# Block products in all four feed-forward blocks, beside the modulation's sums, and the sums over h in mid-turn

## The reference

```
mod = c_act @ mod_w[i] + mod_b[i]                    # 9 rows of 1024 per layer: shift, scale, gate
h = modulate(rmsnorm(x, ffn_norm_w[i, 0]), sh1, sc1)
g, u = jnp.split(h @ w_gu, 2, axis=-1)               # w_gu: 1024 x 5632, so 2816 gate and 2816 up columns
x = x + FFN_HALF * g1[:, None, :] * ((jax.nn.silu(g) * u) @ w_down)
```

## Time and profile before

| | |
|---|---|
| median of 3 runs | 2077.13 (2076.99 to 2077.41) |
| profiled execution, its own time | 2075.79 |
| its span, first to last instruction | 2074.0 |
| TensorE busy | 2056.9 (99% of the span) |
| VectorE busy | 1286.6 (62%) |
| ScalarE busy | 840.3 (41%) |
| DMA | 300.66 MB, mean 145 GB/s |

### The profile page before, as it was taken

One profiled execution on the slowest core, in us unless ns is written; L12 is line 12 of the kernel. 1 busy time (PEld: TensorE's weight loads), 2 busy tenths in 40 slices (PEclk: granted clock), 3 DMA queues, 4 the chain that ended last, 5 costly groups with the idle time before them and its releaser, 6 DMA issues.

```text
span 2074.0 us, 28876 instructions
## 1 busy us (share of the span) xinstructions
PE 2056.9 (99%) x11146; PEld 1741.0 (84%) x11146; DVE 1286.6 (62%) x1985; ACT 840.3 (41%) x1317; POOL 5.6 (0%) x34
## 2 busy tenths in 40 slices
PE   9999999999999999999999999999999999999998
PEld 6888888987878888888888988988888788899887
DVE  6555566687877755555566677664237975766433
ACT  4232222367667743322222344333125843434221
POOL 0000000000000000000000000000000000000000
PEclk9999999999999999999999999999999999999999
DMA  8455566444344323355467533334331113333322
GB/s 336 181 192 202 197 239 234 141 136 136 117 119 140 107 82 120 145 202 194 182 235 247 197 113 102 102 102 151 104 110 61 55 61 122 102 102 141 123 92 72
DMA packets 84253, 300.66 MB, mean 145 GB/s; under 512 B 9008, under 2 KB 11952, under 8 KB 82480
## 3 DMA queue, kind: packets, MB, share of 16 engines
q1 hardware_dynamic: 83856, 299.01, 42.1%
q10 hardware_dynamic: 288, 0.13, 0.0%
HBM read 292.68 MB, written 6.42 MB: 144 GB/s over the span
## 4 chain that ended last, share of the span: by engine, by line
PE 96%; DVE 2%; DMA 1%; ACT 0%; SPq 0%; issue 0%; DVEq 0%; ACTq 0%
PE bank L259 30%; PE bank L261 30%; PE bank L260 30%; PE bank L1223 1%; DMA raw<-w_stream 1%; PE bank L1878 1%; PE bank L1232 1%; PE bank L1913 1%; PE bank L1893 1%; PE bank L1227 1%; DVE x_trunk L859 0%; DVE w_lo_sb L254 0%; PE bank L1214 0%; PE bank L1211 0%; PE bank L388 0%
## 5 line engine op out<-in xcount | busy, mean ns | idle before, releaser
L259 PE MATMUL bank<-h_hi,w_hi_sb 128*128 128x512 f32 (+1 forms) x1924 | 711.4, 370 | 5.9 <-DVE w_lo_sb L254 4.7
L260 PE MATMUL bank<-h_lo,w_hi_sb 128*128 128x512 f32 (+1 forms) x1924 | 702.8, 365 | 0.0
L261 PE MATMUL bank<-h_hi,w_lo_sb 128*128 128x512 f32 (+1 forms) x1924 | 702.8, 365 | 0.0
L254 DVE TENSOR_TENSOR w_lo_sb<-raw,w_hi_sb 128x1024 fp32r<-128x1024 f32 (+1 forms) x326 | 387.1, 1195 | 119.5 <-ACT w_hi_sb L249 119.3
L259 PEld LDWEIGHTS bank<-h_hi,w_hi_sb 128*128 128x128 f32 x1924 | 363.0, 189 | 70.9 <-DVE w_lo_sb L254 6.8
L261 PEld LDWEIGHTS bank<-h_hi,w_lo_sb 128*128 128x128 f32 x1924 | 362.8, 189 | 59.0
L260 PEld LDWEIGHTS bank<-h_lo,w_hi_sb 128*128 128x128 f32 x1924 | 363.2, 189 | 56.3 <-issue 0.2
L249 ACT ACTIVATE w_hi_sb<-raw 128x1024 fp32r<-128x1024 f32 (+1 forms) x326 | 326.1, 1028 | 146.8 <-PE bank L261 142.0
L259 PE MATMUL bank<-a_hi,w_hi_sb 128*128 128x512 f32 (+1 forms) x912 | 324.1, 355 | 0.0
L261 PE MATMUL bank<-a_hi,w_lo_sb 128*128 128x512 f32 (+1 forms) x912 | 323.4, 355 | 0.0
L260 PE MATMUL bank<-a_lo,w_hi_sb 128*128 128x512 f32 (+1 forms) x792 | 289.4, 365 | 0.0
(11 more groups left out here) (263 smaller groups left out, 2139.1 us busy)
## 6 DMA issues: line engine op xcount, KB each, us to landing
raw<-w_stream SPq DMA_DIRECT2D x356, 512.0 KB, 3.6
mod_raw<-w_mod SPq DMA_DIRECT2D x144, 512.0 KB, 4.4
sums<-sums_rows SPq DMA_DIRECT2D x7, 1024.0 KB, 9.2
decays<-decay_rows SPq DMA_DIRECT2D x8, 768.0 KB, 4.0
first_mod<-w_mod SPq DMA_DIRECT2D x10, 512.0 KB, 15.5
x_rows<-x_trunk SPq DMA_DIRECT2D x4, 1024.0 KB, 4.9
x_trunk<-x_rows SPq DMA_DIRECT2D x4, 1024.0 KB, 6.6
first_mod<-w_first SPq DMA_DIRECT2D x3, 1024.0 KB, 18.6
```

The source lines that it names most:

```text
L254: nc.vector.tensor_tensor(w_lo_sb[:, s, 0:width], raw[:, s, 0:width], w_hi_sb[:, s, 0:width], ALU.subtract).then_inc(w_lo, 1)
L259: nc.tensor.matmul(ps, s_hi, m_hi, start=start, stop=False)
L260: nc.tensor.matmul(ps, s_hi, m_lo, start=False, stop=False)
L261: return nc.tensor.matmul(ps, s_lo, m_hi, start=False, stop=stop)
```

## The change

All four blocks get blocked turns: blocks 0 and 1 from turn 4 to turn 9, six turns each, with the mod_blocks at the places `blocks(0)` to `blocks(3)`. `token_whole` moves into the middle of a turn, behind that turn's first two `prep_lo`. In blocks 2 and 3 it stays in the same turn, and `token_sums` goes to the middle of the turn after it. In blocks 0 and 1 they stand in the middle of turns 1 and 2. Blocks 0 and 1 now also store x and fetch it back; the fetch stands in `gu_turn(9)`, behind the first slab load and the first modulation load. The loops of these blocks are written out turn by turn, and the gate and up slabs of the blocked turns are stored in the order that blocked turns read (gate 1, gate 0, up 0, up 1).

```diff
-BLOCKED_FROM = {2: 2, 3: 3}
+BLOCKED_FROM = {0: 4, 1: 4, 2: 2, 3: 3}
...
         def token_whole(dve, k):
             t0 = BLOCKED_FFN.index(k)
             dve.wait_ge(x_put, 32 * (t0 + 1))
+            dve.wait_ge(h_lo_ready, (h_before[0] + 8, h_before[2] + 16, h_before[4] + 8, h_before[6] + 16)[k])
...
                 elif k in BLOCKED_FROM and i == BLOCKED_FROM[k] - 1:
                     preps(0, True)
+                    if mod0 is None:
+                        token_sums(dve, k)
                     leave(0)
                     sum_s3(dve, k, n0, i + 1)
...
                 else:
                     preps(0, True)
+                    if k in BLOCKED_FROM and i == BLOCKED_FROM[k] - 2 - int(mod0 is not None):
+                        token_whole(dve, k)
+                    if k in BLOCKED_FROM and i == BLOCKED_FROM[k] - 2 and mod0 is not None:
+                        token_sums(dve, k)
                     leave(0)
...
                     turn(i, v, part, first)
-                    if i == BLOCKED_FROM[k] - 2:
-                        token_whole(dve, k)
-                        token_sums(dve, k)
...
+            def slabs_and_mods(k, n0, m0, made):
 
                 def gu_turn(i, blocks):
                     for u in range(2):
                         for q in range(2):
                             load_slab(sp, 4 * i + (n0 + 2 * u + q), (n0 + 2 * u + q) % RING)
                             if blocks:
-                                load_mod(sp, 4 * i + (m0 - 4 * halved + 2 * u + q), q)
-
-                if halved:
-                    gu_turn(0, False)
-                with sp.Fori(int(halved), 2 * MOD_GU + int(halved)) as i:
+                                load_mod(sp, 4 * i + (m0 - 4 + 2 * u + q), q)
+                            if i == BLOCKED_TO - 1 and u == q == 0:
+                                fetch_x(k)
+
+                gu_turn(0, False)
+                put_x(made)
+                for i in range(1, 2 * MOD_GU + 1):
                     gu_turn(i, True)
```

More of the change, by code:

```diff
@@ L2218, in _, with put_x, fetch_x @@
                 load_slab(sp, n, n % RING)
-            def slabs_and_mods(n0, m0, halved):
+            x_flat = x[:, :, :].rearrange("p j t -> p (j t)")
+            x_halves = (slice(0, DT * T // 2), slice(DT * T // 2, DT * T))
+            def put_x(made):
+                sp.wait_ge(t_ready, made)
+                for w in x_halves:
+                    sp.dma_start(x_rows[:, w], x_flat[:, w]).then_inc(x_put, 16)
+            def fetch_x(k):
+                sp.wait_ge(part_done, 6 * blocked_before(k, BLOCKED_TO))
+                sp.wait_ge(x_put, 32 * (BLOCKED_FFN.index(k) + 1))
+                for w in x_halves:
+                    sp.dma_start(x_flat[:, w], x_rows[:, w]).then_inc(x_back, 16)
+            def slabs_and_mods(k, n0, m0, made):
                 def gu_turn(i, blocks):
@@ L2227, in gu_turn @@
                             if blocks:
-                                load_mod(sp, 4 * i + (m0 - 4 * halved + 2 * u + q), q)
-                if halved:
-                    gu_turn(0, False)
-                with sp.Fori(int(halved), 2 * MOD_GU + int(halved)) as i:
+                                load_mod(sp, 4 * i + (m0 - 4 + 2 * u + q), q)
[4 more added lines that the diff above has]
+                for i in range(1, 2 * MOD_GU + 1):
                     gu_turn(i, True)
-                if not halved:
-                    gu_turn(2 * MOD_GU, False)
                 def down_turn(i, last):
@@ L2247, in slabs_and_mods @@
                     down_turn(i, i == 1)
-            x_flat = x[:, :, :].rearrange("p j t -> p (j t)")
-            x_halves = (slice(0, DT * T // 2), slice(DT * T // 2, DT * T))
-            def put_x(made):
-                sp.wait_ge(t_ready, made)
-                for w in x_halves:
-                    sp.dma_start(x_rows[:, w], x_flat[:, w]).then_inc(x_put, 16)
-            def fetch_x(k):
-                sp.wait_ge(part_done, 6 * blocked_before(k, BLOCKED_TO))
-                sp.wait_ge(x_put, 32 * (BLOCKED_FFN.index(k) + 1))
-                for w in x_halves:
-                    sp.dma_start(x_flat[:, w], x_rows[:, w]).then_inc(x_back, 16)
             def slabs(n0, n1):
@@ L2273, in _ @@
             sp.dma_start(ssm_rows[:, :], ssm_rows_in.partition_broadcast(P)).then_inc(ssm_loaded, 16)
-            slabs_and_mods(6, 8 * mods0 + 2, True)
+            slabs_and_mods(0, 6, 8 * mods0 + 2, h_before[0] + 8)
             for n in range(S_IN + 6, S_OUT + RING):
@@ L2296, in _ @@
                 load_mod(sp, 8 * mods1 + m, m)
-            slabs_and_mods(S_FFN1 + 6, 8 * mods1 + 2, True)
+            slabs_and_mods(1, S_FFN1 + 6, 8 * mods1 + 2, h_before[2] + 16)
             sp.wait_ge(mod_step, 8 * NMOD)
```

## The result

The change makes the kernel slower: 2106.54 as the median of 4 runs (2103.69 to 2108.37), beside 2077.18 for the kernel before (4 runs, 2076.99 to 2077.41). The ratio is 1.014, with a 95% interval from 1.0127 to 1.0154. The profiled execution took 2108.37, 1.8 above the median; its span is 2106.6.

What follows compares the result with a forecast made beforehand. TensorE set the pace before; in blocked turns VectorE, waiting for late loads, was to. Two blocks +23.8, sums over h -5.6, clock +4: +22.2 on 2077.1 gives 2099.3; range 2088 to 2109, the forecast's own range 2096 to 2104.

Steps and rivals of the forecast that it cites:

- The sums over h: Blocks 2 and 3: with token_sums in mid-turn, the turns of 24.57 and 24.58 fall to 21.76, 5.63 less.
- Which loads are late, and why: Blocked turns, blocks 0 and 1: first and fourth mod_block loads queue behind slab loads that wait for a split.
- turns 5 to 8: Blocks 0 and 1: each takes 22.8, which is 1.0 above the plain turn it replaces.
- VectorE's work of 18.1: VectorE's instructions in a blocked turn with four mod_blocks, which alone would fit into TensorE's 20.98.
- The size of the two waits: Each blocked turn, VectorE: 2.7 ahead of the fourth mod_block, 2.0 ahead of the first, with loads landing after 4.1.
- My bound for landings of 4.6, 2109: Upper bound: ten turns with two waits each longer by 0.5, +10 in all.
- the rival with slower loads: Loads in blocked turns take 4.6 and more to land, total 2109 to 2120; chance 10%.
- Turn 4: First blocked turn of blocks 0 and 1: entered late, TensorE loses 2.8 on 20.98, so 23.8.
- Turn 9: Last blocked turn, blocks 0 and 1: fourth modulation load lands late behind the fetch; 27.5, TensorE idle for 5.7.
- The six pieces: Turn 9's queue: the fetch (four times 512 KB), a slab and a modulation load, 1.28 each, 7.7.
- The clock: TensorE's clock falls ahead of turn 10 in blocks 0 and 1, costing 2 each, 4 in all.
- the one in which the loads are hidden: Operands arrive before their mod_blocks, VectorE's work fits into 20.98, the fetch costs nothing; total 2062; chance 8%.

Runs made afterwards that it cites:

- e1_sums_only: Against the changed kernel, blocks 0 and 1 stay plain; only the sums over h of blocks 2 and 3 move to mid-turn; 2070.38.
- e3_mods_first: Changed kernel with each modulation load ahead of its slab load in SyncE's queue, the fetch of x left in place; 2068.2.
- e6_warm: Changed kernel plus 36 small unused matmuls on TensorE ahead of turn 10 of blocks 0 and 1; 2110.95.
- e9_warm_half: Changed kernel plus 18 small unused matmuls on TensorE ahead of turn 10 of blocks 0 and 1; 2108.24.
- e2_fetch_late: Changed kernel with the fetch of x moved behind the load of turn 9's fourth mod_block; 2096.64.
- e7_turn4: Changed kernel with modulation loads ahead of slab loads, fetch behind turn 9's fourth modulation load, turn 3's third and turn 4's second mod_block earlier; 2062.54.
- e8_more_work: Changed kernel with modulation loads before slab loads, later fetch, and five unused VectorE additions per blocked turn of blocks 0 and 1; 2086.27.
- e10_three_more: Changed kernel with modulation loads before slab loads, later fetch, and three unused VectorE additions per blocked turn of blocks 0 and 1; 2069.44.

## Why the prediction was right, and where its sizes were off

The time, 2106.5, lies in the range, 7.2 above the forecast and 2.5 above its own range, 2096 to 2104. For the profiled execution I had 2098.0, and it took 2108.4.

**The sums over h**: -5.6 forecast. Both turns went to 21.76 in the kernel after and in e1_sums_only, which with its batch's median of 2077.05 for the kernel before gained 6.7 (5.3 between the profiled executions, 2075.8 and 2070.5). Right.

**Which loads are late, and why**: right. The waits stand ahead of the first and the fourth mod_block, they vanish when the loads change places with the slab loads, and turns 5 to 8 then take 20.98. VectorE's work of 18.1 measured 18.34 (turn 7 of e3_mods_first).

**The size of the two waits**: this is the term that was mis-sized, by the landing of 4.1. The ten loads that the first and fourth mod_blocks of turns 4 to 8 wait for landed after 4.3 to 5.5 in the second block (4.65 in the mean) and after 4.5 to 6.3 in the first (5.3). My bound for landings of 4.6, 2109, and the rival with slower loads were nearer to this than the 4.1. In the second block part of it is made good, since the load is issued 1.6 after the split's start, where I had 1.9: the two waits of a turn are 4.9 together beside 4.7. Its turns 5 to 8 took 22.64, 23.53, 23.16 and 23.98, or 93.3 beside 91.2. The longer waits and the 0.24 of VectorE's work make 1.8 of these 2.1.

In the first block they took 24.46, 25.54, 24.15 and 23.27, or 97.4: 6.2 more than forecast. Of the two loads, that for the first mod_block is the late one in turns 4 to 7: it lands after 5.8 to 6.3, and the waits are 1.2 to 1.8 longer than 2.0. In turns 5 to 7 that is 4.4; the fourth mod_block's waits, 0.3 longer, make 1.2 in four turns and VectorE's work 1.0: 6.6 together, which covers the 6.2. I had argued that pairs of loads don't come close together in a blocked turn. They do: the pairs behind `lo_s` and behind `lo_x` are issued at 1004.94 and 1007.36, 2.4 apart. But it is so in both blocks, and in turns 4 to 6 the slab ahead is late too (5.1 to 5.4), with nothing issued just before it. In turns 4, 5 and 6 the trace has 15 of the 16 parts of that load there after 4.4 to 4.5, as in turn 8, and the last after 6.0 to 6.3, so one of the 16 DMA engines is behind. It is no accident of one execution: the same load of turn 6 lands after 7.3 in e6_warm and 7.2 in e9_warm_half, though after 5.4 in e2_fetch_late. In turn 6 a packet of the instruction queue was moved in the ten microseconds around it, and none around turn 8; but there was one around the second block's turn 7 as well, whose load landed after 4.6. **What holds up that engine stays open.**

**Turn 4**: 23.8 forecast, 25.9 and 24.05 measured. The first block's load landed after 6.25 there, and the clock fell (below). In e2_fetch_late, e6_warm and e9_warm_half, where that load landed after 4.7 to 5.1 and the clock stayed, the same turn took 24.1 to 24.5.

**Turn 9**: 27.5 forecast with 5.7 of idle time, 27.1 and 26.2 measured with 4.8 and 4.7. The mechanism is right (e2_fetch_late). The six pieces took 8.0 in both blocks, from the landing of the third mod_block's load (257.2 and 1064.8) to that of the fourth's (265.2 and 1072.8), where I had 7.7. The term that was off is what stands behind the mod_block: I counted both splits, 4.2 in all, but TensorE starts turn 10 with the first of them, 3.1 after the mod_block's start. The second split is paid in turn 10 instead (below). The Trainium skill ("DMA: Bandwidth & Descriptors", Bandwidth), by whose 341 GB/s the six would have taken 9.2, is thus farther off at this place than the rows' 410 GB/s.

**The clock**: it fell ahead of turn 10 in the first block, as forecast, and 0.5 into it in the second. I had 2.0 for each. That number came from counts of matmuls at the start, 6 and then 11 in a microsecond; the granted clock of those windows in the earlier trace rows reads 1.00 in both, so they don't show the level themselves. Where the clock stayed (e2_fetch_late, first block of e9_warm_half), turn 10 still took 22.25 to 22.3, since its second split comes late. So the clock cost 24.7 - 22.3 = 2.4 and 23.6 - 22.3 = 1.3: 3.7 beside 4. With the late split turn 10 was 0.8 over the forecast in the two blocks together. That the 4 fits so well is in part luck, since the two losses were of different size. But I had also said that the clock stays at 1.00 within the turns, because I took 0.7 and 1.1 for the waits there, less than the 2.06 of the earlier trace rows. In the first block the late landings made them 2.82 and 2.16, and the clock fell. By the windows from 131 to 135 TensorE lost 0.5 + 0.5 + 0.5 + 0.2 there (0.2 less for its idle part), and 1.7 from 182 to 186; the waits of 0.9 ahead of the second up tile are gone in these two turns, so that 0.6 and 0.8 remain. In e2_fetch_late the same came once, in turn 5. The Trainium skill ("TensorE: Matmul & The Clock Gate", Part 1) has an idle TensorE throttled to half rate until it has worked for a while; by that rule, these windows agree with their 0.50. Comparing lengths of idle time, as I did, doesn't decide it: 1.93 lowered the clock in e2_fetch_late, and 2.06 in the kernel before did not. Nor did 3.02 in turn 6 of e9_warm_half, longer than any that lowered it within a turn of the kernel after. A row of TensorE's timeline there, and the window behind it:

```profile
179.96 0.47 PE L259 MATMUL bank<-h_hi,w_hi_sb 128*128 128x512 f32 x1 [3.02 <-DVE w_lo_sb L254]
```

```profile
180.00:181.00 1.00, 1.00 (x5) 1.00 0.30 29
```

**The difference summed up** for the profiled execution: first block, turns 4 to 9, 7.9; second block 1.1; turns 10, 0.8; turn 0 of the first block, which varies between executions (30.53 here, 29.98 before), 0.55. That is 10.4, all of it.

**The rivals**: the one in which the loads are hidden and the time is 2062 isn't this kernel, but it is e7_turn4, at 2062.5. The changed kernel lies between the forecast and the rival with slower loads, which began at 2109, and the slower landings of that rival are in it.

## What to carry to other kernels

Work that is moved beside other work must bring its loads with it: in an in-order queue a load that stands behind a load that waits is as late as that one, however free its own slot is. Count the engine's work first, then what each wait may add before the turn is full (here 2.6, so that one late load was nearly free and two cost 1.7 to 3.0 a turn in the second block), and look at the order of the queue before giving up the change. Put a long transfer behind the last small load that somebody needs, not ahead of it.

## What the runs showed of the hardware

- An idle time of two microseconds amid full work can lower TensorE's clock, and its length alone doesn't tell: 1.93 (e2_fetch_late), 2.08 (e8_more_work), 2.16 and 2.82 did, while 2.06 in the kernel before, 2.05 in e10_three_more, 1.74 in the kernel after and 3.02 in e9_warm_half did not. The fall can come when the engine is at work again: it waited until 181.18, and the clock fell between 182 and 183. In e9_warm_half it waited until 1074.59, and the clock was at 0.54 from 1076 on.
- Small float32 matmuls of 128x128 appear as two in the records: 36 calls show as x72 and take 8.20, or 0.11 for each record.
- One of the 16 parts of a load can be 1.5 to 1.8 later than the last of the other 15, and the load lands with it. A modulation load of 512 KB landed 4.1 after its issue in the kernel before, and after 4.5 and 6.3 in turns 8 and 6 of the first block of the kernel after. The DMA share of turns 4 to 8 is only 0.46 to 0.54: the mean share says little of how long a single load takes.
